# Attention scores from stacked rows that pass through memory, in a two-layer decoder on one core

## The reference, cut to what matters

```python
# forgetting attention, 6 heads ("FOX"): c is the running sum of log forget gates
s = q @ k.T * 64 ** -0.5 + c[:, None] - c[None, :]
p = softmax(where(k_pos <= q_pos, s, -1e30));  o = p @ v
# differential attention, 4 heads ("DIFF"): two maps of width 32 per head
s_m = q_m @ k_m.T * 32 ** -0.5 - slope * (q_pos - k_pos)      # m = 0, 1, masked the same way
a = softmax(s_0) - lam * softmax(s_1);  o = rms_norm(a @ v) * g * (1 - lam_init)
# all heads and the SGU side by side, then one projection
y = concat(fox, diff, sgu) @ w_out
```

## Time and profile before

| | |
|---|---|
| median of 3 runs | 2105.26 us |
| lowest and highest run | 2099.78 and 2107.17 us |
| the profiled execution, whole | 2098.93 us |
| its span, first to last instruction | 2097.2 us |
| mean granted PE clock | 0.979 of full |
| matmuls | 9631 |

### The profile page before, as it was taken

The page is one execution under the profiler, slowest core; times in us unless marked ns, Lnnn a source line. Parts: engine busy times, 40 slices in busy tenths (PEclk is TensorE's granted clock), DMA queues, the critical chain, the costliest instruction groups (busy, mean ns, idle before and its releaser), DMA issues.

```text
span 2097.2 us, 27179 instructions
## 1 busy us (share of the span) xinstructions
PE 2030.1 (97%) x9631; PEld 1675.1 (80%) x9631; DVE 1121.5 (53%) x1807; ACT 732.3 (35%) x1033; POOL 271.1 (13%) x240
## 2 busy tenths in 40 slices
PE   7999999999998999999999999999999989999996
PEld 6888888887777888888778888888777778888885
DVE  6444544574566744444574444456656575453446
ACT  4323332444433433333243333324434342333321
POOL 5000000321102400000050000004211033000002
PEclk9999999999989999999999999999999899999998
DMA  5223223131101223222222223222310012222221
GB/s 214 100 80 120 86 94 120 69 111 70 41 21 40 101 80 120 100 80 102 110 101 80 100 80 120 100 100 89 121 41 21 21 61 100 106 79 115 100 100 40
DMA packets 27427, 185.34 MB, mean 88 GB/s; under 512 B 4192, under 2 KB 4320, under 8 KB 5344
## 3 DMA queue, kind: packets, MB, share of 16 engines
q1 hardware_dynamic: 27360, 184.50, 23.9%
HBM read 182.39 MB, written 2.10 MB: 88 GB/s over the span
## 4 chain that ended last, share of the span: by engine, by line
PE 85%; DVE 6%; issue 6%; POOL 2%; ACT 1%; DMA 0%; DVEq 0%; SPq 0%; POOLq 0%; ACTq 0%
PE bank L774 74%; PE bank L912 5%; PE bank L975 2%; PE bank L990 1%; PE bank L1001 1%; POOL res L462 1%; DVE res L1188 1%; PE bank L1003 1%; DVE st L1212 1%; DVE nat L1334 1%; PE bank L802 1%; DMA rawA<-in_a_w 0%; PE bank L926 0%; PE bank L976 0%; DVE hl L1262 0%
## 5 line engine op out<-in xcount | busy, mean ns | idle before, releaser
L774 PE MATMUL bank<-whiD,hl 128*128 128x512 f32 x1408 | 443.3, 390 | 3.2 <-DVE hl L1262 2.7
L1188 DVE SCALAR_TENSOR_TENSOR res<-bank,res 128x512 f32<-128x512 f32 x384 | 259.0, 688 | 168.4 <-PE bank L774 166.3
L774 PEld LDWEIGHTS bank<-whiD,hl 128*128 128x128 f32 x1408 | 264.3, 188 | 61.1 <-DVE hl L1262 4.4
L774 PE MATMUL bank<-xhi,whiA 128*128 128x512 f32 (+1 forms) x768 | 289.1, 376 | 14.9 <-DVE xlo L1167 14.9
L774 PE MATMUL bank<-xlo,whiA 128*128 128x512 f32 (+1 forms) x768 | 287.4, 374 | 0.0
L774 PE MATMUL bank<-xhi,wloA 128*128 128x512 f32 (+1 forms) x768 | 287.3, 374 | 0.0
L774 PE MATMUL bank<-wloD,hl 128*128 128x512 f32 x704 | 273.9, 389 | 0.0
L774 PE MATMUL bank<-xhi,whiB 128*128 128x512 f32 x704 | 273.9, 389 | 0.0
L774 PE MATMUL bank<-xlo,whiB 128*128 128x512 f32 x704 | 273.9, 389 | 0.0
L774 PE MATMUL bank<-xhi,wloB 128*128 128x512 f32 x704 | 273.9, 389 | 0.0
L774 PEld LDWEIGHTS bank<-xhi,whiA 128*128 128x128 f32 x768 | 146.9, 191 | 42.1 <-DVE xlo L1167 17.2
(11 more groups left out here) (174 smaller groups left out, 3200.8 us busy)
## 6 DMA issues: line engine op xcount, KB each, us to landing
rawA<-in_a_w SPq DMA_DIRECT2D x63, 1024.0 KB, 4.8
rawB<-in_b_w SPq DMA_DIRECT2D x54, 1024.0 KB, 4.8
rawD<-in_d_w SPq DMA_DIRECT2D x46, 1024.0 KB, 4.8
gbr<-in_gb_row SPq DMA_DIRECT2D x7, 1024.0 KB, 6.7
out<-nat SPq DMA_DIRECT2D x4, 512.0 KB, 2.6
mixr<-in_mix_row SPq DMA_DIRECT2D x2, 515.0 KB, 10.4
nat<-in_x SPq DMA_DIRECT2D x1, 1024.0 KB, 7.2
res<-in_x SPq DMA_DIRECT2D x1, 1024.0 KB, 11.0
```

Of the source, the lines that this page charges most:

```text
L774: ins = t_.matmul(out_, a_, b_, start=(start and k == 1), stop=(stop and k == n), skip_group_check=check)
L1188: v.scalar_tensor_tensor(out=r, in0=bank[b][:, :], scalar=scale, in1=r, op0=ALU.mult, op1=ALU.add).then_inc(step, 1)
```

## The change

- **Stacked scores.** Query and key parts of four groups of 32 rows (a quarter of a pair each: half of a FOX head, or one map of a DIFF head) are written to a tensor `stacks` in memory, and read back as tiles of 97 rows: rows 0 to 31, 32 to 63 and 64 to 95 hold (q hi, q hi, q lo) against (k hi, k lo, k hi), row 96 a one-row bias (-1 against c or against the scaled positions). One matmul of 97 rows does the work of three and the bias. A FOX step issues two of them (its 64 rows are two groups) and the mask, a DIFF step one and the mask for each map. The mask is in fp32r now.
- **Transport.** For each pair SP issues 12 DMAs of 64 KB for the query and 12 for the key; once at the start 18 bias rows; in each layer 12 rows of c, between pair 0's query and key. POOL reads the stack of each head back (`load_stack`, 776 KB in two DMAs) into the tiles of `whi["D"]` and `wlo["D"]`, after the last scores of the same head number of the pair before.
- **Order of pairs**: FOX, DIFF, FOX, DIFF, FOX. Projections run two pairs ahead: pairs 0 and 1 are projected before the first scores; the fillers of pairs 0 to 2 are projections, those of pairs 3 and 4 the early output part, always three matmuls each. A pair's key is split in step 0, its query in step 4 (before, both in step 7).
- **Output projection**: four early chunks (7, 0, 5, 6), four late ones (3, 1, 4, 2). Their D weights are split after the last scores of each stack, by ACT and POOL. Splits of the output weights go from DVE to POOL.
- **Layer boundary**: the last output of layer 0's second feed-forward block is held back too, its first chunks are started early, and the norm's gain is scaled earlier.
- Loops over layers and pairs are unrolled in the program.

```diff
+ROWS = 32
+STACK = 3 * ROWS + 1
+EARLY = [(7, "B", 0), (0, "B", D), (5, "A", 0), (6, "A", D)]
+LATE = [(3, "D", 0), (1, "D", D), (4, "B", 0), (2, "B", D)]
...
+                def put(b, tile, order, put_ok):
+                    for s in range(4):
+                        for j, part in enumerate(order):
+                            sp.dma_start(stacks[b, s // 2, j * ROWS:(j + 1) * ROWS, tile + s % 2, :],
+                                         part[s * ROWS:(s + 1) * ROWS, :].bitcast(F32)).then_inc(put_ok, 16)
+                for b in range(BODIES):
+                    sp.wait_ge(qk_ok, (l * BODIES + b) * 2 + 1)
+                    put(b, 0, (qhi, qhi, qlo), q_put)
+                    if b == 0:
+                        sp.wait_ge(c_ok, l + 1)
+                        for h in range(FOX_H):
+                            for j in range(2):
+                                sp.dma_start(stacks[h // 2 * 2, h % 2, STACK - 1:STACK, 2 + j, :],
+                                             brow[32 * j + h:32 * j + h + 1, :].bitcast(F32)).then_inc(c_put, 16)
+                    sp.wait_ge(qk_ok, (l * BODIES + b) * 2 + 2)
+                    put(b, 2, (khi, klo, khi), k_put)
+                    fill("A", l * A_ALL + A_QK + b + 2)
...
+                def load_stack(b, h):
+                    n = l * BODIES + b + 1
+                    pool.wait_ge(q_put, 16 * 12 * n)
+                    pool.wait_ge(k_put, 16 * 12 * n)
+                    if b:
+                        G = (b - 1) * STEPS + (h + 1) * NT - 1
+                        pool.wait_ge(s_done[1 if is_diff(G) else 0], count(l, G, 1 if is_diff(G) else 0))
+                    else:
+                        pool.wait_ge(y_done, (l * Y_ALL + Y_WO) * 8 + AHEAD)
+                    for lo, hi in ((STACK - 1, STACK), (0, STACK - 1)):
+                        g.dma_start(stack[h][lo:hi, :, :], stacks[b, h, lo:hi, :, :]).then_inc(stacked[h], 16)
...
-                        product(bank[i][:, 0:n_], [((qhi[r:r + rows, t * P:t * P + P], qlo[r:r + rows, t * P:t * P + P]),
-                                                    (khi[r:r + rows, 0:n_], klo[r:r + rows, 0:n_]))], stop=False)
-                        t_.matmul(bank[i][:, 0:n_], sel[0:65, hh, :], brow[0:65, 0:n_], start=False, stop=False)
-                        t_.matmul(bank[i][:, t * P:n_], identb[:, :], maskb[:, :], start=False, stop=True).then_inc(s_done[m], 1)
+                        for n in (range(2) if maps == 1 else (m,)):
+                            t_.matmul(bank[i][:, 0:n_], tile[0:STACK, n, t * P:t * P + P], tile[0:STACK, 2 + n, 0:n_],
+                                      start=(n == 0 or maps == 2), stop=False)
+                        t_.matmul(bank[i][:, t * P:n_], identr[:, :], maskr[:, :], start=False, stop=True).then_inc(s_done[m], 1)
...
+                for G in range(ALL):
+                    b, k = divmod(G, STEPS)
+                    if k == 0 and b <= EARLY_BODY:
+                        between = early(l) if b == EARLY_BODY else project(l, b + 2)
+                    scores(G)
+                    next(between, None)
+                    if G >= 1:
+                        turn_p(G - 1)
+                    next(between, None)
+                    if b == BODIES - 1 and k in LATE_TURNS:
+                        turn_y(l, LATE_TURNS[k])
+                    if G >= 2:
+                        values(G - 2)
...
+                    row_max(G)
+                    if G and not is_diff(G - 1):
+                        inverse(G - 1)
+                    if is_diff(G):
+                        mix(G)
+                    if G:
+                        p_lo(G - 1)
+                    if k == 0 and b + 1 < BODIES:
+                        key(b + 1)
+                    if k == NT and b < EARLY_BODY:
+                        query(b + 2)
...
+                    if G >= 2:
+                        output(G - 2)
```

734 lines of the change are left out of this document (382 added, 352 removed).

## The result

| | before | after |
|---|---|---|
| median | 2102.52 us (4 runs, 2098.74 to 2107.17) | 2079.88 us (4 runs, 2069.76 to 2084.54) |
| span of the profiled execution | 2097.2 us | 2073.6 us |
| mean granted PE clock | 0.979 | 0.974 |
| matmuls | 9631 | 9341 |

What follows compares the result with a forecast made beforehand. PE was taken to bound the kernel before. From 2098.9 us, 12.6 came off for both layers' attention and 7 for the boundary, giving 2079; 4 added for run spread made 2083, own range 2060 to 2104, with rivals 2040 to 2125.

Steps and rivals of the forecast that it cites:

- PE bound before, products worth 65 us: Attention scores: PE is the bound, and fewer products save it 32.6 us per layer, 65 us for both.
- DIFF pairs bound by DVE and ACT: DIFF pairs: PE work falls to 25 us, but DVE and ACT hold the pair at 31.5 us.
- PE stays the bound: Rival, chance 0.15: DVE overlaps its steps better, DIFF pairs fall to 25 us, total 2045, or 2027 with fast first loads.
- The second DIFF pair: Second DIFF pair of a layer: four y splits, two adds and the transposes' waits for them make it 37.5 us.
- What PE waits for: PE's gaps in DIFF pairs: ended by DVE, values waiting for p_lo and transposes for the mix; 6.5 us idle per pair.
- FOX pairs at 24: FOX pairs: 26 us less 3.8 of products, plus 1.8 for the new order of splits and outputs, make 24 us.
- The way through memory: Ahead of each layer's first pair: puts, landing and loads bring first scores at 494 (bounds 485 to 502); PE idles 13 us.
- puts at 0.9 us: Rival, chance 0.17: a put takes 0.9 us rather than 0.46, first scores come 16 us later per layer, total 2115.
- The page cited: Transport: by the skill's page a head's load takes 3.8 us, and 12 puts one after the other 11.4 us.
- The clock: Attention: 10 us of half clock left per layer, which costs 5 us.
- The rival in which the clock makes the kernel slower: Chance 0.15: PE does less in DIFF pairs and falls to half clock, costing 11.5 us a pair, total 2129.
- The boundary: Layer boundary: one held output and early first chunks remove 4.5 us of idleness and most of 3.4 us of half clock: -7.

Runs made afterwards that it cites:

- diff_more: The changed kernel with each 97-row product of a DIFF map issued four times instead of once, output the same: 2076.13 us, ratio 0.9877.
- before_fewer: The kernel before with as many score instructions as the changed one, third product part (DIFF: first two) and bias left out, nothing stacked: 2048.17 us, ratio 0.9754.
- crows_act: The changed kernel with the 12 rows of c issued from ACT's queue, behind pair 1's query, instead of SP's: 2079.65 us, ratio 0.9896.
- output_sooner: The changed kernel with DVE taking output(G-2) ahead of mix(G) in DIFF steps: 2081.09 us, ratio 0.9906.
- no_way: The changed kernel without puts, rows of c, stack loads or the wait for them, scores taken from whatever the tiles hold: 2045.26 us, ratio 0.9727.
- hold: The changed kernel with SP holding back everything after pair 0's key puts until head 0's stack has landed: 2077.05 us, ratio 0.9874.
- boundary: The changed kernel without the held output of layer 0's last block and the norm's early chunks; earlier gain scaling stays: 2080.32 us, ratio 0.9886.
- two_queues: The changed kernel with pair 0's key puts issued by ACT, norm parameters fetched behind pair 1's puts, and redundant PE products in waits: 2062.44 us, ratio 0.9819.

## Why the prediction was right

**The total**: 2083 predicted, 2080 measured, faster as the likeliest case said. Several terms were off, in both directions, so that a total within 3 us is in part luck.

- **PE bound before, products worth 65 us.** Right: the score groups took 110.9 us, as worked out (12 x 3.9 and 8 x 7.9 make 110), and lost 70. The 97-row product had no row; four of them at 512 keys in `diff_more` follow each other by 0.25 us, for which 0.23 was taken.

```profile
525.73 1.18 PE L1098 MATMUL bank<-whiD 97*128 97x512 f32 x4
526.74 0.23 PE L1100 MATMUL bank<-maskr,identr 128*128 128x128 f32 x1
```

- **DIFF pairs bound by DVE and ACT.** Right in mechanism: `diff_more`, 7.4 us of products for 1.3 to 2.1 us of time. The step at 384 keys is 3.76 us where 3.9 was predicted. The pair was mis-sized: 28.3 us for 31.5. The subtraction began from a stretch of 39 us, of which the pair itself, from first mask to first mask, is 37.7, and took only the named waits of DVE out. In the old order `before_fewer` has 29.8 us, with DVE busy for 23.0 where it was 24.1 before, since passes that don't wait overlap a little; the changed kernel has 28.5 with 21.0, the selector's cast and the pair's last mix having left the stretch. So DVE overlapped its steps somewhat better than rows 4 let one see. That was the condition of the rival "PE stays the bound", met in part.
- **The second DIFF pair.** 37.5 us predicted, 37.3 and 36.9 measured, and this is luck: y's splits and the adds were to make it long, but 20.5 us of it lay at half clock in each layer, and at a clock of 0.95 the same steps take 33.1 (`crows_act`).
- **What PE waits for.** Wrong. I named the low half of P and the mix; the trace names the outputs in the bank which the transposes write to. `output_sooner` shows that this is one ring: moving the output passes ahead exchanged a wait for ACT of 5.9 us for one for PE of 6.2.
- **FOX pairs at 24.** Pair 0 took 21.7 us, pair 2 26.2 (30.1 in layer 1, with 6.8 us at half clock); pair 2 carries the first DIFF pair's norm and the same bank wait. The mean of layer 0 is right, neither value is.
- **The way through memory.** Every link was there. SP's issue: 0.46 us predicted and 0.457 measured for 64 KB, 0.32 for the rows. The puts were there at 484.8, where 486.4 was predicted. The load was the term mis-sized: 7.8 us allowed, 11.6 and 9.5 measured, 8.5 to 10.4 in other kernels with the same way; first scores at 498.3, within the bounds 485 to 502 but over the value of 494. The rival "puts at 0.9 us" didn't occur. PE's wait was 15.2 and 14.0 us for 13 predicted. `no_way` prices the whole at 35 us.
- **The page cited.** The Trainium skill (DMA: Bandwidth & Descriptors, Anatomy of one DMA) gives 3.8 us for a head's load by its 2.0 us and 436 GB/s. The trace differs: 5.8 us with head 1's load and a weight slot beside it (`hold`), 8.5 to 11.6 with the norm rows and puts as well, and the measurement decides. No run here has the load alone. By the same page's Bandwidth section, whose 0.95 us is for loads of 128 partitions issued from POOL, 12 puts one after the other would have taken an estimated 11.4 us; SP issued 12 in 5.49 and the last landed 1.8 us later, so they didn't run one after the other.
- **The clock.** I left 10 us of half clock per layer, which costs 5. In the attention alone it took 28 us over both layers, 14 each. This is the term furthest off. It was hidden: the first DIFF pairs were 3 us shorter than predicted, and the second ones had as much allowed for other things as the clock took. So the mixers gained more than predicted, 11.1 and 9.6 us for 6.3. The rival in which the clock makes the kernel slower didn't occur. (Its price of 11.5 us a pair isn't 45 less 31.5, which is 13.5; it comes out near that only if the clock's share already in the 2083 is taken off.)
- **The boundary.** 7 predicted, 3.8 measured, and `boundary` shows that the two mechanisms I gave for it bring 0.4, within the scatter. The step that failed is the reading of PE's gaps there as caused by the output that wasn't held back. PE's clock was 1.00 from 1028 to 1060 us after, 0.95 with that part undone, so the clock's half of the term exists but is small.

**Where the gain went.** By the medians: 54 us from the first 54 us of products, 3 from the next 16 with all the rest (2048 to 2045), and those at the layer boundary, 35 lost to the transport. The net is 22 us.

## What to carry over

Cutting the work of a bound engine pays up to the next ring of waits, and the order of the other engines within one step, read from the trace before, tells where that is. A long wait of PE costs twice, as waiting and as a lower clock around its end; redundant products put into it kept the clock up, but weren't shown to make this kernel faster by themselves. An edit that moves a wait from one place to another shows nothing in the total, so read where it went. Compare the same stretch in several kernels that share its code before you put a number on an edit: here the head load alone lay between 8.5 and 11.6 us. A chain through memory is paid in full by the first stage that needs it: count its issues, keep large loads out from between its small transfers and their landing, and look at what queues behind any wait added to hold them back.

## What the hardware showed

- A long wait lowers PE's clock. It was at 0.52 for the 16 us up to and around the first scores, with a wait of 15.2 us in them; with the wait filled it stayed at 1.00. With 30 us of redundant products in the DIFF pairs (`diff_more`), the kernel wasn't slower, 2076 for 2080. But idleness isn't all: before, the second DIFF pair's stretch had a clock of 0.87 with PE busy for 52.5 of 53 us, and `before_fewer`, with 10 us more idle time in the attention, lost 6 us less to the clock. What lowers it there isn't shown.
- A store of 2 KB took 4.66 us to land when a load of 1 MB had been issued a us earlier in another queue (`crows_act`), and puts of 64 KB took 4.8 to 5.6 us in the same case (`two_queues`, both layers), where a put otherwise takes 1.7. A load of 768 KB took 5.8 us beside the other head's and a weight slot, and 8.5 to 11.6 with 1 MB of norm rows and the puts there too, at 275 GB/s in all (the stretch 485 to 501 after).
- POOL can hold up DVE: a mix of two operands in SBUF took 2.47 us instead of 0.35 beside POOL's subtraction, in both layers of `output_sooner`. The Trainium skill (SBUF — State Buffer, SBUF: two separate sides) describes this as a pair of ports that one of them holds for a whole instruction, for DVE operations with two SBUF inputs among others; the trace agrees, as DVE's passes with an operand in an accumulator bank ran beside the same split undisturbed (0.27 and 0.28 us at 524.0 to 524.6, with the split from 523.99 to 526.36).
